# Expert gather of a PEER layer: four picks of one head for 32 tokens in each gather, in place of one pick for 128 tokens

## The reference: what is computed

```python
def peer(x, w_pq, subkeys, pu, pv):
    qp = (x @ w_pq).reshape(T, 8, 2, 128)
    s = jnp.einsum('thcd,hcnd->thcn', qp, subkeys)
    s1, i1 = lax.top_k(s[:, :, 0], 16); s2, i2 = lax.top_k(s[:, :, 1], 16)
    cand = s1[..., :, None] + s2[..., None, :]          # 16 x 16 pairs of each head
    top_s, sel = lax.top_k(cand.reshape(T, 8, 256), 16)
    eidx = ...                                           # expert number of each pick, of 16384
    g = jax.nn.softmax(top_s, axis=-1)
    u, vv = pu[eidx], pv[eidx]
    a = jax.nn.gelu(jnp.einsum('thkd,td->thk', u, x))
    return jnp.einsum('thk,thkd->td', g * a, vv)
```

## Time and profile before

| | |
|---|---|
| median of 3 runs (lowest to highest) | 1436.56 us (1431.0 to 1441.49) |
| time of the profiled execution | 1436.09 us |
| its span | 1434.3 us |
| PE busy | 1172.1 us (82%) |
| DVE busy | 893.0 us (62%) |
| POOL busy | 469.4 us (33%) |
| ACT busy | 141.8 us (10%) |
| gathers: bytes, share of 16 DMA engines over the span | 402.68 MB, 70.2% |

### The profile page before, as it was taken

One profiled execution on the slowest core, in us unless ns is written; L12 is line 12 of the kernel. 1 busy time (PEld: TensorE's weight loads), 2 busy tenths in 40 slices (PEclk: granted clock), 3 DMA queues, 4 the chain that ended last, 5 costly groups with the idle time before them and its releaser, 6 DMA issues.

```text
span 1434.3 us, 10516 instructions
## 1 busy us (share of the span) xinstructions
PE 1172.1 (82%) x3320; PEld 589.7 (41%) x3320; DVE 893.0 (62%) x2323; ACT 141.8 (10%) x304; POOL 469.4 (33%) x417
## 2 busy tenths in 40 slices
PE   7999999999999987787757858777776778778777
PEld 4545655677665533232322323333332223233332
DVE  4006445839467988788788795555555555555555
ACT  2101201221100100001010000000001000000000
POOL 0001121000435344343434424335443344344432
PEclk9999999989999998898878888989888998889989
DMA  8321547250899898998979999999998999999996
GB/s 314 122 69 62 95 120 299 89 235 1 317 377 369 361 422 339 395 384 340 395 304 385 395 374 366 406 397 388 395 397 329 414 400 378 397 395 398 402 409 257
DMA packets 68823, 454.85 MB, mean 317 GB/s; under 512 B 7240, under 2 KB 14764, under 8 KB 17328
## 3 DMA queue, kind: packets, MB, share of 16 engines
q0 software_dynamic: 55296, 402.68, 70.2%
q1 hardware_dynamic: 12656, 48.60, 9.9%
q10 hardware_dynamic: 832, 3.08, 0.7%
HBM read 446.62 MB, written 7.71 MB: 317 GB/s over the span
## 4 chain that ended last, share of the span: by engine, by line
PE 52%; DMA 27%; DVE 14%; issue 4%; ACT 2%; POOL 1%; SPq 0%; DVEq 0%; POOLq 0%
PE ps L1035 28%; DMA arena<-in_peer_uv,arena 26%; PE ps L769 7%; DVE arena L1471 4%; PE ps L775 4%; PE ps L1027 3%; PE ps L889 2%; PE ps L1009 2%; POOL arena L558 1%; DVE arena L1479 1%; DMA arena<-in_w_out 1%; ACT arena L698 1%; PE ps L982 1%; DVE arena L1228 1%; DVE arena L1450 1%
## 5 line engine op out<-in xcount | busy, mean ns | idle before, releaser
L1035 PE MATMUL ps<-arena 128*128 128x512 f32 x1536 | 771.0, 662 | 234.1 <-DVE arena L1479 232.7
L558 POOL DMA_INDIRECT arena<-in_peer_uv,arena x384 | 441.1, 1149 | 751.1 <-PE ps L1035 579.4
L1471 DVE CUSTOM_DVE_ANT_0 arena<-arena 128x1024 f32<-128x1024 f32 x376 | 454.0, 1224 | 282.5 <-DMA arena<-in_peer_uv,arena 281.9
L1035 PEld LDWEIGHTS ps<-arena 128*128 128x128 f32 x1536 | 318.4, 213 | 681.5 <-issue 403.4
L769 PE MATMUL ps<-arena 128*128 128x384 f32 (+1 forms) x336 | 114.0, 498 | 0.0
L698 ACT ACTIVATE arena<-arena 128x4 f32<-128x4 f32 x94 | 19.3, 205 | 852.0 <-DVE arena L1471 852.0
L1479 DVE TENSOR_SCALAR arena<-arena 128x128 f32<-128x128 f32 x376 | 83.5, 297 | 3.3
L769 PEld LDWEIGHTS ps<-arena 128*128 128x128 f32 (+1 forms) x336 | 64.4, 195 | 45.5 <-issue 4.1
L775 PE MATMUL ps<-arena 128*128 128x512 f32 x144 | 62.5, 592 | 0.0
L1027 PE MATMUL ps<-arena 128*128 128x256 f32 x256 | 56.2, 379 | 0.9 <-ACT arena L587 0.9
L587 ACT ACTIVATE arena<-ps 128x512 f32<-128x512 f32 (+2 forms) x63 | 30.6, 511 | 247.7 <-PE ps L1027 78.0
(11 more groups left out here) (232 smaller groups left out, 664.4 us busy)
## 6 DMA issues: line engine op xcount, KB each, us to landing
arena<-in_w_in SPq DMA_DIRECT2D x8, 2048.0 KB, 7.7
arena<-in_w_pq SPq DMA_DIRECT2D x4, 2048.0 KB, 9.9
arena<-in_peer_uv,arena POOLq DMA_INDIRECT x384, 9.2
arena<-in_w_out SPq DMA_DIRECT2D x3, 1024.0 KB, 7.1
arena<-in_state_C ACTq DMA_DIRECT2D x1, 2064.0 KB, 11.3
out_new_C_s<-arena SPq DMA_DIRECT2D x1, 2064.0 KB, 6.6
arena<-in_cache_k SPq DMA_DIRECT2D x4, 512.0 KB, 7.0
arena<-in_cache_v SPq DMA_DIRECT2D x1, 2048.0 KB, 17.5
```

The costliest lines, as they stand in the source:

```text
L558: nc.gpsimd.indirect_dma_start(slots[s], None, d["peer_uv"], bass.IndirectOffsetOnAxis(ap=eidx[:, t, e:e + 1], axis=0)).then_inc(landed[s] ...
L1035: last = mm(ps[:, BANKS + half, :], diag[:, s, :], slots[s][:, DM + 512 * half:DM + 512 * half + 512], start=first and s == 0, stop=final ...
L1471: last = v.tensor_tensor_reduce(slots[s][:, 0:DM], slots[s][:, 0:DM], hn[:, t, :], 1.0, 0.0, ALU.mult, ALU.add, aslot[:, s:s + 1])
```

## The change

- A "quad" is four consecutive gathers. Gather j of a quad takes four picks of one head for the tokens 32j to 32j+31: partition 32i + r holds pick i of token 32j + r. The number of gathers and their rows stay the same (`gathers`, `QUAD`, `BLOCK`).
- So that the dot product meets the right token, SP copies the normed token vectors of a tile into four arrays `hn4` in which 32 tokens stand four times: 16 DMAs of 32 x 1024 floats a tile (`copies`), for the first tile before its gathers, for the others later.
- The expert numbers and the gates are brought into the same layout once for each half tile: PE multiplies by a copying matrix `rep` into PSUM (`place` on PE), DVE copies out blocks of 32 partitions (`place` on DVE). The part's first gather waits for this.
- POOL makes, for each quad, the identity blocks of 32x32 times the gates (`eyegate`, one instruction of 128x128). ACT takes the gelu of four columns and then scales four blocks of 128x32 by it (`diag`). DVE has only the dot products left.
- PE multiplies with stationary blocks of 32 columns: the four slots of a quad go to four 32-column tiles of the array, each to its own 32 partitions of the sum (`weigh`). The four slots are released together behind the second half.
- Buffers: 7 for the first 72 gathers, 11 from then on, the last four of which had held query weights (`slot_after`, "qq15").
- The order is written anew: `query_steps` and `routing_steps` are by rounds of two quads up to round 31; all loops are written out. The final gains `gfin` are loaded later.

The diff, cut to its core:

```diff
-SLOTS = 8
+QUAD = 4
+QUADS = HK // QUAD
+GATED = 3
+EARLY_SLOTS, LATE_SLOTS = 7, 11
+EARLY = 72
...
+    held = [i % EARLY_SLOTS if i < EARLY else (i - EARLY) % LATE_SLOTS for i in range(NT * HK)]
...
-        slot_after = ["y11"] * 4 + ["qq3"] * 2 + ["qq7"] * 2
+        slot_after = ["y11"] * 3 + ["qq3"] * 2 + ["qq7"] * 2 + ["qq15"] * 4
... SP
+            def copies(n):
+                for j in range(QUAD):
+                    for i in range(QUAD):
+                        sp.dma_start(arena[BLOCK * i:BLOCK * i + BLOCK, hn4_at[n % 2][j]:hn4_at[n % 2][j] + DM],
+                                     hn[BLOCK * j:BLOCK * j + BLOCK, ORDER[n], :]).then_inc(hn4_in[n], 16)
+            sp.wait_ge(hn_ok, NT)
+            was_read(sp, "y11")
+            copies(0)
+            filled(sp, "qq15")
+            sp.dma_start(gfin, d["g_fin"].partition_broadcast(P)).then_inc(gfin_in, 16)
+            filled(sp, f"sc{ORDER[0]}3")
+            copies(1)
+            store(0)
+            sp.wait_ge(used, HK)
+            copies(2)
... POOL
+            for q in range(NT * QUADS):
+                n, m = divmod(q, QUADS)
+                part, k = divmod(q, QUADS // 2)
+                if k == 0:
+                    pool.wait_ge(idx_ok, QUAD * (part + 1))
+                for i in range(QUAD * q, QUAD * q + QUAD):
+                    b = held[i]
+                    if earlier[i]:
+                        pool.wait_ge(used, max(k for k in range(i) if held[k] == b) + 1)
+                    else:
+                        filled(pool, slot_after[b])
+                    nc.gpsimd.indirect_dma_start(
+                        slots[b], None, d["peer_uv"],
+                        bass.IndirectOffsetOnAxis(ap=idxT[:, part, i % QUAD, k:k + 1], axis=0)).then_inc(landed[b], 16)
+                nc.gpsimd.tensor_tensor(eyegate[:, q % GATED], over(eye, 1, QUAD), over(gm[:, part, :, k], 2, BLOCK),
+                                        ALU.mult).then_inc(eg_ok, 1)
... ACT
+            def gelus(q):
+                act.wait_ge(a_ok, QUAD * q + QUAD)
+                act.activation(gslot[:, q % 2, :], aslot[:, q % (16 // QUAD), :], ACT.Gelu_apprx_tanh).then_inc(ge_ok, 1)
+                act.wait_ge(ge_ok, q + 1)
+                act.wait_ge(eg_ok, q + 1)
+                for j in range(QUAD):
+                    act.activation(diag[:, q % 2, j, :], eyegate[:, q % GATED, j, :], ACT.Copy,
+                                   scale=gslot[:, q % 2, j:j + 1]).then_inc(diag_ok, 1)
... PE
+            def weigh(q):
+                m = q % QUADS
+                pe.wait_ge(diag_ok, QUAD * q + QUAD)
+                for half in range(2):
+                    for j in range(QUAD):
+                        last = mm(ps[BLOCK * j:BLOCK * j + BLOCK, ACC + half, :], diag[:, q % 2, j, :],
+                                  slots[held[QUAD * q + j]][:, DM + 512 * half:DM + 512 * half + 512],
+                                  start=m == 0, stop=m == QUADS - 1, skip_group_check=True)
+                        if half:
+                            last.then_inc(used, 1)
+            place(0)
+            for q in range(NT * QUADS):
+                ... the round's query matmuls, one half of them in each of its two quads
+                weigh(q)
+                if step == PER - 1 and r in steps and steps[r][0] == "experts":
+                    place(steps[r][1])
... DVE
+            def experts(q):
+                for j in range(QUAD):
+                    i = QUAD * q + j
+                    rows = slots[held[i]][:, 0:DM]
+                    dve.wait_ge(landed[held[i]], 16 * (earlier[i] + 1))
+                    v.tensor_tensor_reduce(rows, rows, hn4[q // QUADS % 2][j], 1.0, 0.0, ALU.mult, ALU.add,
+                                           aslot[:, q % (16 // QUAD), j:j + 1]).then_inc(a_ok, 1)
```

More of the change, by code:

```diff
@@ L98, in psum_plan @@
         add("A", f"hnT{t}0", f"hnT{t}1")
-    for what, *k in sum(query_steps(), []):
-        add("V" if what == "sc" else "A", what + "".join(map(str, k)))
+    add("V", "ix0", "gx0")
+    queries, routing = query_steps(), routing_steps()
+    for i in range(NT * ROUNDS):
+        for what, *k in queries.get(i, []):
+            add("V" if what == "sc" else "A", what + "".join(map(str, k)))
+        if i in routing and routing[i][0] == "experts":
+            add("V", f"ix{routing[i][1]}", f"gx{routing[i][1]}")
     return plan
@@ L399, in bank @@
             return ps[:, index[name] % BANKS, :]
+        where = gathers()
+        held, earlier = slot_buffers()
         chunk_slot = {c: c % 3 for c in range(9)} | {11: 2, 12: 1, 13: 3, 14: 4}
@@ L1028, in prompt_query, with place @@
                 end(last)
-            def weigh(n, i, first, final):
-                for s in range(SLOTS):
-                    pe.wait_ge(diag_ok, (n * ROUNDS + i) * SLOTS + s + 1)
-                    for half in range(2):
-                        last = mm(ps[:, BANKS + half, :], diag[:, s, :], slots[s][:, DM + 512 * half:DM + 512 * half + 512],
-                                  start=first and s == 0, stop=final and s == SLOTS - 1, skip_group_check=True)
-                    last.then_inc(used, 1)
+            def weigh(q):
[8 more added lines that the diff above has]
+                            last.then_inc(used, 1)
+            def place(part):
+                for k, what in enumerate(("ix", "gx")):
+                    b = begin(f"{what}{part}")
+                    pe.wait_ge(dup_ok, 2 * part + 1 + k)
+                    t, h0, n = PARTS[part]
+                    for j in range(QUAD):
+                        src = (gates[:, t] if k else ef[:, 0])[:, h0:h0 + n].rearrange("p h k -> p (h k)")
+                        last = mm(b[:, PK * n * j:PK * n * j + PK * n], rep[:, j, :], src, start=True, stop=True)
+                    end(last)
             pe.wait_ge(hn_ok, 1)
@@ L1059, in _ @@
             was_read(pe, f"hnT{ORDER[-1]}1")
-            for i in range(ROUNDS):
-                for what, *k in query_steps()[i]:
+            pe.wait_ge(rep_ok, 1)
+            place(0)
+            queries, steps = query_steps(), routing_steps()
+            for q in range(NT * QUADS):
+                r, step = divmod(q, PER)
+                jobs = queries.get(r, [])
+                half = (len(jobs) + 1) // 2
+                for what, *k in jobs[half * step:half * step + half]:
                     if what == "qq":
@@ L1481, in last_experts @@
[L1481 to L1492 removed]
+                v.engine_nop().then_inc(dup_ok, 1)
@@ new lines, in place @@
+            def place(part):
+                for what, out in (("ix", idxT), ("gx", gm)):
+                    filled(dve, f"{what}{part}")
+                    src = bank(f"{what}{part}")[:, 0:QUAD * 4 * PK].rearrange("p (j k i) -> p j k i", j=QUAD, i=QUAD)
+                    for i in range(QUAD):
+                        r = slice(BLOCK * i, BLOCK * i + BLOCK)
+                        last = v.tensor_copy(out[r, part], src[r, :, :, i])
+                        if what == "ix" and i < QUAD - 1:
+                            last.then_inc(idx_ok, 1)
+                    done(last)
+                    was_read(dve, f"{what}{part}")
+                    v.engine_nop().then_inc(idx_ok if what == "ix" else gm_ok, 1)
```

225 lines of the change are left out of this document (97 added, 128 removed).

## The result

| | before | after |
|---|---|---|
| median of 4 runs (of before one more than shown ahead) | 1433.78 us | 1453.42 us |
| lowest to highest | 1428.14 to 1441.49 | 1453.24 to 1457.95 |
| ratio, 95% interval | | 1.0141, 1.0086 to 1.0196 |
| span of the profiled execution | 1434.3 | 1451.4 |

The change makes the kernel slower by 1.4%. The time lies inside the stated range (1400 to 1455), but above the forecast's own range (1412 to 1445), and slower by over 1% had been given 0.17.

A forecast was written before the change was run, and what follows sets the result against it. Taking the gathers' DMA as near the bound, it put gather 72's dot at 632.6 us, added 771.3 for 311 gathers and 7.5 for transfers, then the tail: span 1425.4, forecast 1427 us, range 1400 to 1455.

The forecast's parts named there:

- the forecast's own range: Whole kernel: 1412 to 1445 us, from issue-to-dot times of 5.5 to 6.5 us and copies up to twice their price.
- the copies: Added token-vector transfers: second tile's with moved gains 6.2 us in the early part, third tile's 5.0 in the late one.
- the routing steps: Late part: VectorE's 10.1 us steps cost nothing because queued gathers cover them; uncovered, some 5 us each.
- The start: First gather at 363.7 us, second quad's last dot at 415.8, later queries waiting behind the first quad: 28 us lost.
- The early loop: Seven-buffer part: 6.4 us from last dot to next issue plus 6.0 issue to dot, 12.4 us a quad.
- The late rate: Eleven-buffer part: gathers every 2.48 us, 771.3 us for 311; rival that the rate does not rise: 1505 us, chance 0.05.
- The drain and the tail: Everything drains once before gather 72, 6.4 + 5.8 us; after the last dot, 6.4 and 7.6 us to the end.
- overlap in pairs: Slower rival, PE's weighing: the four tiles overlap only in pairs, a 7.3 us burst, 1485 us in all; chance 0.10.
- its high clock: Faster rival, early part: PE stays at its high clock, loop 1.9 us shorter, 1404 us in all; chance 0.25.
- the case of unseen stalls: Stalls of DVE or POOL not seen in the profile, ending above 1445 us; chance 0.05.
- signs of being wrong: Changed profile: a PE burst over 5 us, late quads above 10.2 us, or an early loop of 11 us.
- the forecast's own case: Whole kernel: the summed forecast of 1427 us with its spread, chance 0.55; of it 0.18 faster, 0.36 same.

The follow-up runs named there:

- order: Changed kernel with TensorE's queries 0 to 3 ahead of the first placement, queries 4 to 7 behind it and ahead of the first weighing: 1429.98 us.
- place1: Changed kernel with the later placements on TensorE one quad later, behind the next quad's weighing: 1448.47 us.
- nocopy: Changed kernel without the token-vector copies of tiles 1 and 2, whose dot products read tile 0's copies: 1429.69 us.
- e70: Changed kernel with the eleven late buffers beginning at gather 70 instead of gather 72: 1447.63 us.
- late8: Changed kernel with 8 late buffers instead of 11, nothing else: 1531.71 us.

## Why the prediction was wrong

The step that failed is the price of what was added and of what has no cover: the copies, taken at 10 us for the bytes alone, cost 24; the routing steps, taken "at nothing", cost 7 in the early part; and the late part, taken as an even stream, is some 9 us longer than that. The other mechanisms of the forecast were right. The loop adds 2, and 7 came back by an earlier start.

- **The start** was right to the tenth: 52.1 us from the first gather to the second quad's last dot, as 415.8 - 363.7 had said, and `order` shows that TensorE's order causes it. The first gather came at 357.0 and not 363.7, although the placement took 3.65 us and not 1.9: the first routing ended 7.9 us earlier than in the profiled execution of the kernel before. In the seven profiled executions with this start the first gather came between 355.7 and 361.5; why the program ahead of it is quicker, and differs so much, was not looked for.
- **The early loop** of 12.4 us a quad was nearly right. The twelve quads of 2 to 17 with no long step or copy beside them (all but 9, 11, 12 and 13) take 12.6 on average: 6.37 from the fourth landing to POOL's issue into the buffers that this quad gives back (forecast 6.4) and 6.27 from there to the data (forecast 6.0). One such quad in the kernel after:

```profile
473.47 1.23 DVE L1562 CUSTOM_DVE_ANT_0 arena<-arena 128x1024 f32<-128x1024 f32 x1 [2.94 <-DMA arena<-in_peer_uv,arena]
474.74 0.20 ACT L762 ACTIVATE arena<-arena 128x4 f32<-128x4 f32 x1 [3.14 <-DVE arena L1562]
...
475.99 3.19 PE L1098 MATMUL ps<-arena 128*32 128x512 f32 x16 [4.81 <-ACT arena L768]
...
479.44 0.94 POOL L620 DMA_INDIRECT arena<-in_peer_uv,arena  x1 [5.58 <-PE ps L1098]
...
485.79 1.23 DVE L1562 CUSTOM_DVE_ANT_0 arena<-arena 128x1024 f32<-128x1024 f32 x1 [2.10 <-DMA arena<-in_peer_uv,arena]
```

- **The copies were mis-sized**: "6.2 us in the early part at 423 GB/s, the third's 5.0 in the late one", 10.0 without the gains; leaving them out gave 24.1 in the trace, 11.1 and 13.0. The remark that reading and writing SBUF at once could double them stood in the prediction but went into the forecast's own range only, and even the doubled price is short of this. The prediction had no row for a copy from SBUF to SBUF beside gathers, took the lower bound, and should have taken a higher one: these 14 us are the largest part of the miss.
- **Routing steps "at nothing"** was written of the late part; in the early one, where seven buffers give little cover, they were not priced at all. Quad 9, beside a step of pairs, took 14.7 us, and quad 11 took 17.3, of which `place1` gave back 3.0: with the 12.6 of the others, some 7 us in all. That TensorE stands in a placement until the experts step ends was seen at the start and not looked for again.
- **The late rate** was right: 9.94 us a quad in most quads, 2.485 a gather. The Trainium skill, page HBM Reference, section Specifications (TRN2), says that a core streaming alone measures about 425 GB/s; the trace agrees with 422 in its slices. The 358 GB/s that the prediction weighed is given there as the share with both cores of a pair streaming. Without the copies, `nocopy` still takes 783.2 us from the dot of gather 72 to the last; the forecast had 771.3 and 2.5 for stores. Some 9 us are left: 1.6 are the 2.485 against 2.48, the others lie in stalls of about a microsecond beside routing steps and of more at the tiles' ends; which of them costs what was not tried.
- **The drain and the tail** were right: 12.7 against 12.2, and 13.9 against 14.0. But the hole of the drain is worth only 7 us when filled (`e70`); why not more is not shown.
- **The rivals.** The four tiles overlap nearly fully: bursts of 16 passes mostly take 3.2 to 3.65 us, and 1.92 at the higher clock, where overlap in pairs had been priced at 7.3 and 3.6. PE did not keep its high clock: 0.69 is granted on average in the early part, and two of its eighteen bursts took 1.92 us. What happened is nearest to the case of unseen stalls, which had 0.05, and its place was not VectorE or POOL alone but the DMA's copies.

Gain and loss were said nearly to cancel, so the sign hung on small terms: counted to the true dot of gather 72, 56 us lost and 68 won became 65 and 50. That the time still fell into the stated range is owed to its width, not to the sum. Of the signs of being wrong that the prediction gave, none appeared (bursts up to 3.65 us, most late quads 9.94, the early loop 12.6), and it had named none for the copies or the routing steps. Faster had 0.40 and slower 0.17. Of the forecast's own case only 0.01 went to slower, although the added transfers could only lengthen the stage and stood in the sum at their lower bound.

## What to carry to other kernels

Price an added SBUF-to-SBUF copy beside a saturated DMA at more than twice its bytes (24 us for 4.2 MB here), and ask whether an engine with idle time can make it: with TensorE and ScalarE making these the kernel took 1430.01 us, with none made 1429.69. When buffers are handed back several at a time, count what is still in the air meanwhile: 8 buffers in fours gave 370 GB/s, 8 one by one in the kernel before 388, 11 in fours 420. And where a change moves work into a queue ahead of what another engine waits for, the order inside that queue can be worth the whole difference: here 23 us by the medians, where the change had lost 20.

## What the runs showed of the hardware

- The 32 copies of 128 KB beside gathers (tiles 1 and 2) cost the 16 DMA engines 17 us where their bytes alone take 10 at 423 GB/s, and made the gathers' packets 11 us longer in all (the kernel after against `nocopy`). Meanwhile the DMA share reads 1.02 at 336 GB/s: a full share is no full rate.
- Sixteen small matmuls (128x64) took 3.65 us behind a wait of 11.62 us, at a granted clock of 0.50 (1.2 GHz; the kernel after), and 1.89 us directly behind 8.8 us of queries, at 1.00 (2.4 GHz; `order`). So here a placement ahead of the queries is dearer than the same placement among them.
- The same front part of the program brings the first gather to 355.7 us in one execution (`late8`) and 361.5 in another (`place1`); landmarks are best compared from the first gather on.
